# Order of the last turns and block combinations at the entrance of a float32 feed-forward stage

## What is computed

```python
mix = jnp.einsum('blc,cd->bld', jnp.concatenate([o, y], axis=-1), w_out[l])
h_res = h_res + rms_norm(mix, post_mix_g[l])

h = rms_norm(h_res, pre_ffn_g[l])
f = jax.nn.silu(jnp.einsum('bld,df->blf', h, w_gate[l])) * jnp.einsum('bld,df->blf', h, w_up[l])
f = jnp.einsum('blf,fd->bld', f, w_down[l])
h_res = h_res + rms_norm(f, post_ffn_g[l])
```

## Time and profile before

| | |
|---|---|
| median of three runs | 2554.58 us |
| the profiled execution | 2554.64 us |
| its span, first to last instruction | 2552.7 us |
| TensorE (PE) busy | 2415.6 us, 95% |
| VectorE (DVE) busy | 1473.3 us, 58% |
| ScalarE (ACT) busy | 799.4 us, 31% |
| GpSimd (POOL) busy | 1154.0 us, 45% |
| mean granted TensorE clock | 0.976 |

### The profile page before, as it was taken

One profiled execution on the slowest core, in us unless ns is written; L12 is line 12 of the kernel. 1 busy time (PEld: TensorE's weight loads), 2 busy tenths in 40 slices (PEclk: granted clock), 3 DMA queues, 4 the chain that ended last, 5 costly groups with the idle time before them and its releaser, 6 DMA issues.

```text
span 2552.7 us, 32735 instructions
## 1 busy us (share of the span) xinstructions
PE 2415.6 (95%) x11678; PEld 1956.9 (77%) x11678; DVE 1473.3 (58%) x2113; ACT 799.4 (31%) x1517; POOL 1154.0 (45%) x888
## 2 busy tenths in 40 slices
PE   8997888897999999999999998889989999999997
PEld 7976756676788888888778886778768888888885
DVE  5974766536555655555574302664645655556556
ACT  4231356624222222222241002552532222222222
POOL 3210040353655566555582533001745665556553
PEclk8998899899999999999999998999999999999999
DMA  5445520032111111111242122001311111111114
GB/s 147 125 132 132 174 77 1 7 104 96 42 58 49 58 53 49 49 49 49 91 157 64 50 66 83 10 1 42 131 42 51 59 51 49 49 49 49 49 54 156
DMA packets 176914, 179.28 MB, mean 70 GB/s; under 512 B 39704, under 2 KB 139544, under 8 KB 176816
## 3 DMA queue, kind: packets, MB, share of 16 engines
q1 hardware_dynamic: 171520, 164.02, 21.2%
q10 hardware_dynamic: 5296, 13.96, 1.6%
HBM read 147.46 MB, written 30.49 MB: 70 GB/s over the span
## 4 chain that ended last, share of the span: by engine, by line
PE 83%; DVE 8%; ACT 3%; issue 2%; POOL 2%; DMA 2%; ACTq 0%; SPq 0%; POOLq 0%; DVEq 0%
PE ps L267 23%; PE ps L269 23%; PE ps L268 23%; PE ps L1466 3%; PE ps L1498 3%; PE ps L1484 2%; PE ps L474 1%; DVE hbuf L425 1%; ACT ex L1546 1%; DVE hbuf L2013 1%; PE ps L2737 1%; DVE ex L1577 0%; PE ps L456 0%; DMA msb<-ssm_lags 0%; DVE hbuf L431 0%
## 5 line engine op out<-in xcount | busy, mean ns | idle before, releaser
L2013 DVE TENSOR_TENSOR hbuf<-hbuf,ps 128x1024 f32<-128x1024 f32 x320 | 390.7, 1221 | 245.5 <-PE ps L269 223.7
L267 PE MATMUL ps<-mlp_dh,mlp_fh 128*128 128x512 f32 x672 | 263.8, 393 | 4.9 <-DVE hbuf L2013 4.4
L269 PE MATMUL ps<-mlp_dh,mlp_fl 128*128 128x512 f32 x672 | 263.0, 391 | 0.0
L268 PE MATMUL ps<-mlp_dl,mlp_fh 128*128 128x512 f32 x672 | 262.2, 390 | 0.0
L207 POOL TENSOR_TENSOR wgt<-raw,ones 128x512 fp32r<-128x512 f32 x76 | 87.2, 1147 | 322.6 <-PE ps L269 165.5
L1779 POOL TENSOR_TENSOR mlp_s_raw<-mlp_gh_raw,mlp_s_raw 128x512 f32<-128x512 f32 x44 | 57.2, 1299 | 284.1 <-PE ps L269 284.1
L267 PEld LDWEIGHTS ps<-mlp_dh,mlp_fh 128*128 128x128 f32 x672 | 126.3, 188 | 35.7 <-DVE hbuf L2013 8.2
L269 PEld LDWEIGHTS ps<-mlp_dh,mlp_fl 128*128 128x128 f32 x672 | 126.3, 188 | 27.5
L268 PEld LDWEIGHTS ps<-mlp_dl,mlp_fh 128*128 128x128 f32 x672 | 126.4, 188 | 27.3
L1792 POOL TENSOR_TENSOR mlp_dl<-mlp_d_raw,mlp_dh 128x1024 fp32r<-128x1024 f32 x42 | 114.0, 2713 | 46.5 <-ACT mlp_dh L1991 46.5
L2050 DVE TENSOR_TENSOR mlp_fl<-mlp_p,mlp_fh 128x512 fp32r<-128x512 f32 x42 | 114.4, 2725 | 3.6
(11 more groups left out here) (483 smaller groups left out, 6696.8 us busy)
## 6 DMA issues: line engine op xcount, KB each, us to landing
h<-hbuf SPq DMA_DIRECT2D x24, 512.0 KB, 2.9
mlp_d_raw<-in_w_down SPq DMA_DIRECT2D x21, 512.0 KB, 3.5
mlp_d_raw<-in_w_ffn_out SPq DMA_DIRECT2D x21, 512.0 KB, 3.7
raw<-in_w_in SPq DMA_DIRECT2D x40, 256.0 KB, 2.8
raw<-in_w_out SPq DMA_DIRECT2D x32, 256.0 KB, 2.8
res_b<-h SPq DMA_DIRECT2D x16, 512.0 KB, 4.4
mlp_ul<-in_w_up SPq DMA_DIRECT2D x22, 256.0 KB, 3.0
mlp_uh_raw<-in_w_up SPq DMA_DIRECT2D x22, 256.0 KB, 3.3
```

Source lines behind the costliest of these rows:

```text
L267: pe.matmul(out, lhs[0], rhs[0], start=first, stop=False, skip_group_check=over)
L268: pe.matmul(out, lhs[0], rhs[1], start=False, stop=False, skip_group_check=over)
L269: return pe.matmul(out, lhs[1], rhs[0], start=False, stop=last, skip_group_check=over)
L2013: v.tensor_tensor(self.acc[:, i, :], self.acc[:, i, :], src, ALU.add).then_inc(self.s["added"], 1)
```

## The change

Nothing is computed differently: the same instructions run, in another order, and two banks of one tile change places. Four edits belong together.

1. On TensorE the turns of tiles 5, 6 and 7 come ahead of the combinations of the tile before, the second half product `gh` moves ahead of turn 6, and each `t3` comes later. The last two, (2, 3) and (3, 3), are made behind the product `s1`; `s3` alone waits for (3, 3).
2. On ScalarE `act_keep` moves ahead of the last square (`act_sq2` of tile 7).
3. On ScalarE and VectorE the casts and subtractions of the last tiles follow the new order; `T_ORDER` lists it and the counts come from it.
4. Tile 6 is turned into banks (2, 1) and not (1, 2), so that (2, 1) and (2, 3) stand in bank 1, which `s2` needs, and (2, 2) in bank 2, which `s1` needs.

```diff
         def t_count(self, j, n):
-            return T_FIRST + 12 * (self.n // 2) + 3 * j + n
+            return T_FIRST + 12 * (self.n // 2) + T_ORDER.index((j, n)) + 1
...
             if begun:
-                begun()
+                begun(0)
...
             down_pair(1)
+            if begun:
+                begun(1)
             self.wait(pe, "taken", f * 5 + 1)
...
             self.pe_product(pe, 0, 0, "gl", self.BX[0], True)
+            turns.pe_turn(pe, 5)
             turns.pe_t24(pe, 0)
-            turns.pe_turn(pe, 5)
+            self.pe_x_second(pe, 0, 0)
+            turns.pe_turn(pe, 6)
             turns.pe_t3(pe, 0)
-            self.pe_x_second(pe, 0, 0)
             turns.pe_t24(pe, 1)
-            turns.pe_turn(pe, 6)
+            turns.t_ready(pe, 0, 3)
+            turns.pe_turn(pe, 7)
             turns.pe_t3(pe, 1)
             turns.pe_t24(pe, 2)
-            turns.t_ready(pe, 0, 3)
-            turns.pe_turn(pe, 7)
-            turns.pe_t3(pe, 2)
             turns.pe_t24(pe, 3)
-            turns.t_ready(pe, 2, 3)
-
-            def rest(pe=pe):
-                turns.pe_t3(pe, 3)
-                turns.t_ready(pe, 3, 3)
+            turns.t_ready(pe, 2, 2)
+
+            def rest(n):
+                if n == 0:
+                    turns.pe_t3(pe, 2)
+                    turns.pe_t3(pe, 3)
+                    turns.t_ready(pe, 2, 3)
+                else:
+                    turns.t_ready(pe, 3, 3)
...
+    T_ORDER = [(j, n) for j in range(2) for n in (1, 2, 3)] + [(2, 1), (2, 2), (3, 1), (3, 2), (2, 3), (3, 3)]
...
-    banks_out = [ring3[i % 3] for i in range(4)] + [(5, 6), (7, 4), (1, 2), (5, 6)]
+    banks_out = [ring3[i % 3] for i in range(4)] + [(5, 6), (7, 4), (2, 1), (5, 6)]
...
+        post[n].act_hi(act, 5)
+        mlp.act_keep(act, 0, 0)
+        post[n].act_sq2(act, 7)
+        post[n].act_t(act, 0, 1)
+        post[n].act_t(act, 0, 2)
+        post[n].act_hi(act, 6)
+        post[n].act_t(act, 0, 3)
+        post[n].act_t(act, 1, 1)
+        post[n].act_t(act, 1, 2)
+        post[n].act_hi(act, 7)
+        for j, t in T_ORDER[5:]:
+            post[n].act_t(act, j, t)
...
+        post[n].dve_t(v, 0, 1)
+        post[n].dve_t(v, 0, 2)
+        post[n].dve_scale(v, 7)
+        post[n].dve_t(v, 0, 3)
+        post[n].dve_lo(v, 6)
+        post[n].dve_t(v, 1, 1)
+        post[n].dve_t(v, 1, 2)
+        post[n].dve_lo(v, 7)
+        for j, t in T_ORDER[5:]:
+            post[n].dve_t(v, j, t)
```

More of the change, by code:

```diff
@@ L2448, in act_beside_out @@
             mlp.act_hi(act, 0, 0, name)
[L2449 to L2455, removed]
+        for i in range(NT):
+            empty(i)
+            step = base + NT + i
+            act.wait_ge(emptied[step % 2], step // 2 + 1)
+            post[n].act_sq(act, i)
+            if i >= 3:
                 post[n].act_hi(act, i - 3)
-            if 0 <= i - 1 < NT:
+            if i >= 1:
                 post[n].act_sq2(act, i - 1)
[L2459 to L2465, removed]
             for name in tasks.get(i, ()):
                 mlp.act_hi(act, 0, 0, name)
+        post[n].act_hi(act, 5)
[10 more added lines that the diff above has]
+            post[n].act_t(act, j, t)
     def dve_beside_out(v, n, total):
@@ L2472, in dve_beside_out @@
         loaded(v, "gb_c", n + 1)
-        for i in range(NT + 5):
+        for i in range(NT + 1):
             if total and i < NT:
                 total(i)
-            if 0 <= i - 1 < NT:
+            if i >= 1:
                 post[n].dve_norm(v, i - 1)
                 post[n].dve_res(v, i - 1)
-            if 0 <= i - 2 < NT:
+            if i >= 2:
                 post[n].dve_scale(v, i - 2)
-            if 0 <= i - 3 < NT:
+            if i >= 3:
                 post[n].dve_lo(v, i - 3)
[L2483 to L2487, removed]
+        post[n].dve_t(v, 0, 1)
[8 more added lines that the diff above has]
+            post[n].dve_t(v, j, t)
     def pool_beside_out(pool, n, mlp):
```

## The result

| | before | after |
|---|---|---|
| median of the runs beside each other | 2554.98 us (4 runs, 2554.26 to 2558.36) | 2525.26 us (4 runs, 2521.40 to 2527.61) |
| profiled execution | 2554.64 us | 2525.80 us |
| its span | 2552.7 us | 2523.8 us |
| mean granted clock | 0.976 | 0.980 |

The ratio is 0.9878, with an interval of 0.9862 to 0.9893: about 31 us less, between 27 and 35. The two medians as they stand differ by 29.7 us. The forecast, 2527.5 us, is a ratio of 0.9894 and lies just outside that interval, too small a gain.

The account below looks back on a forecast made before the run. TensorE, busy 95%, loses time only standing still or at its lower clock. Entrance gains 12.3 (B) + 14.8 (A) = 27.1 us, so 2554.64 - 27.1 = 2527.5 us; forecast 2525 to 2530, range 2524 to 2534.

Parts of the forecast that it names:

- The new schedule: Both entrances laid out step by step from measured lengths: s2 starts 14.8 us earlier in A, 12.3 us in B.
- The waits removed: TensorE's waits in the old order, 12.1 us in entrance A and 10.4 us in B, go.
- The low clock removed: Stretches at 1.2 GHz behind long TensorE waits go: three in A, two in B, 1.6 us each.
- from the other side: Cross-check per entrance: old waits plus low clock less new waits gives 14.75 us in A, 12.2 in B.
- The bounds: Best 2523.9 us if every remaining wait goes; worst 2535.5 us if five stretches still run at the lower clock.
- Hidden costs: GpSimd's sums and the second window's weight loads have room, so set at nothing; swap and ScalarE queueing cost nothing extra.
- Rival 1: In the entrances, remaining small waits still lower the clock: two stretches give 2530.7 us, four 2533.9; chance 0.15.
- Rival 2: The ring of waits closes elsewhere in the entrances, slipping 0.69 us at each tight place: 2531.6 us; chance 0.14.
- the tight places: Turn 7, pe_t3(1) and s1 in each entrance, where a slip by one low costs 0.69 us.
- Rival 3: The 42 later windows run in a worse phase; at 0.8 us each, 2561 us; chance 0.02.
- rival 4: Nothing happens, because the stretch is bound by work and not by order: 2554.6 us; chance 0.02.

Follow-up runs that it names:

- e7: Changed kernel with tile 6 back in banks 1 and 2 and the t3 of (2, 3) ahead of s1: 2525.45 us, ratio 0.9885.
- e8: Changed kernel, swap of banks kept, with the t3 of (2, 3) made ahead of s1: 2523.92 us, ratio 0.9880.
- e6: Changed kernel with ScalarE squaring tile 7 before it copies the sum of gl, as before the change: 2533.66 us, ratio 0.9913.
- e12: Changed kernel with product gh put back behind turn 6 and the t3 of (0, 3): 2531.93 us, ratio 0.9896.
- e5: Kernel before, old order, with matmuls that nobody reads filling TensorE's waits in both entrances: 2545.29 us, ratio 0.9961.
- e2: The changed kernel measured again without any edit, five rounds: 2526.84 us, ratio 0.9883 (0.9868 to 0.9897).
- e1: The kernel before measured again without any edit, as if it were a change: ratio 1.0006 (0.9996 to 1.0016).

## Why the prediction was right, and where it fell short

*The new schedule* was right. It was laid out from lengths in the trace before, and both entrances came out within 0.1 us of it, in three profiles each. In the traces of the variants e7 and e8 came out within 0.1 us of what was expected per entrance, e6 and e12 inside the ranges that were given for them. The waits that it named are there with the size that it gave: 0.6 us before turn 5 in A, 0.25 before `pe_t3(1)`, 1.0 before `s2`.

*The waits removed* were right: 10.4 and 12.2 us in every execution of the old order.

*The low clock removed* is the step that failed: "B has two of them, A three", each 1.6 us, 8.0 in all. I took the number of low stretches from one execution as if it belonged to the program, like the waits. It belongs to the execution: in four of six executions B has a third one. Against e5's full-clock lengths the old entrances lose 5.2 and 4.1 us to the clock on the mean of six, 9.3 together, and 7.4 in the execution that I had; B was at nearly its shortest there. That is where the forecast came out small: 27.1 us is the length of the old entrances in that one execution (72.4) less the schedule's 45.3, and with their mean length (74.3) it is 29.0. It is a mis-sized term of the sum; the mechanism was right. That the check "from the other side" agreed was in part luck: its 8.0 us of clock were 0.6 too many for that execution, and its 18.9 us for the waits 0.9 too few (e5's lengths less the new ones: 19.8).

What is left between 29.1 and the 31 and 29.9 us of the two ratios can't be told from the scatter of the runs; the intervals of both measurements of the change hold 29.1. The second one, e2, also holds the forecast's ratio of 0.9894, so the miss is shown by the traces more than by the times.

*The bounds* repeated the mistake: the lower end came from the waits that were left in the new order (2523.9), and let the old order's clock term stand. With A at up to 40.41 and B at up to 37.13 us the old order can be 5.2 us worse than in my profile, so the gain could reach 32 us in one pair of executions.

*Hidden costs*: set at nothing, and nothing shows in the feed-forward stages. From the first `s2` of A to the last low of that stage (`mlp_fzl<-mlp_p`, 1277.06 us before, 1260.42 after), all 22 windows, it is 644.7 to 644.8 us in each of the fourteen profiled executions, and behind B 681.4 to 681.5. The scatter of A to B, 1202.7 to 1207.0 us, comes in about 930 us behind A, in the second block's attention, where no edit is. There the seven executions with the new A have 1205.4 us on the mean and the six with the old one 1203.9; whether that is more than scatter is not shown.

*The rivals.* Rival 1, the clock falls anyway, did not happen: the granted clock is 1.00 in both entrances of every run of the change, with waits of up to 1.8 us in all, the largest 0.95 us. The rule of the Trainium skill that I had weighed for it ("TensorE: Matmul & The Clock Gate", section "A second HAM failure mode: psum-queue depth-cycling") is not borne out at these sizes. Longer single waits do bring the low clock: in e6 and e12 waits of 2.43 and 1.97 us had low matmuls behind them in A, while waits of 1.06 and 1.55 us in e6's and e7's B did not. These are one execution each, and the 1.8 us wait of the old A had low matmuls behind it in three of six, so no bound follows from them. The Trainium skill says in "TensorE: Matmul & The Clock Gate", section "What's actually happening", that the window in which activity is judged runs freely. The executions of the old order fit that, in that the same waits cost 14 to 28 low matmuls in B. I had not drawn the consequence. Rival 2, a slip at the tight places, did not happen. Rival 3, a worse phase in the windows, is excluded by the 644.7 to 644.8 us above, and rival 4 by the result.

About a third of the gain, 9.3 of 29.1 us, is clock and not waiting. This is shown by e5, which keeps all the waits' time and gets the clock alone.

*The edits by themselves.* Edit 2 is worth 5.2 us (e6), the place of `gh` 3.3 (e12), the swap of banks 0.6 (e7). The rest, the turns ahead of the combinations and the late `t3` with the lists that follow them, was measured only together.

## What to carry to other kernels

A schedule laid out by hand from the lengths in one profile was good to a tenth of a microsecond here; what one profile does not give is how much of the time behind a wait runs at the lower clock, so profile several executions, or reckon a range for that term. Where TensorE turns, ScalarE casts, VectorE subtracts and TensorE needs the result, give TensorE independent work between the turn and the use of the result. And a wait of about 2 us and more on TensorE can cost clock too: here 10.4 and 12.2 us of waits cost 4.1 and 5.2 us more on the mean. When such a wait can't be removed, filling it with matmuls that nobody reads can still pay.

## What the runs showed of the hardware

- Filling TensorE's waits with 79 useless matmuls in all made the kernel 10.0 us faster (e5; 6 to 14 by its interval), at a granted clock of 1.00 in both entrances.
- With the same order and the same 12.2 us of waits, entrance A took between 37.90 and 40.41 us from execution to execution, with 17 to 30 matmuls at the lower clock. Behind the same wait of 2.76 us the clock was 0.50 in e1's B and 1.00 in the first profile's.
- The time of the untouched kernel scatters by more than its first three runs suggested, 2547.3 to 2561.7 us over all its runs but the one of 6055.68. Up to A alone it is 590.3 to 596.5 us over the profiled executions.
